# A two-layer encoder: the tail of each layer as one block per engine, norm root applied to the products, attention head by head

## The reference, cut to what matters

```python
def rms_norm(x, g):
    y = xf * lax.rsqrt(jnp.mean(jnp.square(xf), axis=-1, keepdims=True) + NORM_EPS)
    return y * g
def cross_attention(h, m, w_q, w_kv, w_o):
    q = (h @ w_q).reshape(B, T, XATTN_HEADS, XATTN_HEAD_DIM)
    ...
    p = jax.nn.softmax(einsum('bqhd,bkhd->bhqk', q, k) * (XATTN_HEAD_DIM ** -0.5))
    return einsum('bhqk,bkhd->bqhd', p, v).reshape(B, T, D) @ w_o
...
    h = h + mixed @ w_out                                   # output projection of the mixer
    h = h + cross_attention(rms_norm(h, norm_xattn[i]), rms_norm(mem, norm_mem[i]), ...)
    h = h + jnp.square(jax.nn.relu(rms_norm(h, norm_ffn[i]) @ w_up)) @ w_down
```

## Time and profile before

| | us |
|---|---|
| median of 3 runs | 2164.2 (2164.2 to 2166.83) |
| the profiled execution | 2160.84 |
| its span in the trace | 2158.6 |
| tail of layer 0, from the end of its projection's products (363.14) to the end of the last down product (864.21) | 501.07 |
| the same of layer 1 (1638.37 to 2138.06) | 499.69 |

### The profile page before, as it was taken

The page is one execution under the profiler, slowest core; times in us unless marked ns, Lnnn a source line. Parts: engine busy times, 40 slices in busy tenths (PEclk is TensorE's granted clock), DMA queues, the critical chain, the costliest instruction groups (busy, mean ns, idle before and its releaser), DMA issues. The chain is left out here.

```text
span 2158.6 us, 40341 instructions
## 1 busy us (share of the span) xinstructions
PE 1953.0 (90%) x17897; PEld 1563.9 (72%) x17897; DVE 1092.0 (51%) x1403; ACT 760.1 (35%) x1023; POOL 208.0 (10%) x153
## 2 busy tenths in 40 slices
PE   6899878998999999899968888888688899999998
PEld 4798547766888888667747877888457677888886
DVE  4792554334432432565368787786264425423432
ACT  4422563333321321145543333332253424312322
POOL 1000001000000001220022222222010010000000
PEclk9999989999999999999979999999899999999998
DMA  5224323302233232343211111110423113332320
GB/s 174 85 69 148 120 79 117 98 20 78 92 104 98 79 117 78 116 159 119 101 50 35 36 36 36 35 33 18 165 87 117 59 40 90 105 98 79 97 98 39
DMA packets 153015, 183.76 MB, mean 85 GB/s; under 512 B 9033, under 2 KB 141302, under 8 KB 151306
## 3 DMA queue, kind: packets, MB, share of 16 engines
q1 hardware_dynamic: 148576, 168.28, 23.9%
q0 software_dynamic: 3616, 12.71, 1.5%
q10 hardware_dynamic: 650, 0.19, 0.0%
HBM read 160.18 MB, written 20.99 MB: 84 GB/s over the span
## 5 line engine op out<-in xcount | busy, mean ns | idle before, releaser
L327 DVE TENSOR_TENSOR weights_lo<-w,weights_hi 128x2048 fp32r<-128x2048 f32 x106 | 242.9, 2292 | 299.2 <-ACT weights_hi L314 299.2
L314 ACT ACTIVATE weights_hi<-w 128x2048 fp32r<-128x2048 f32 x110 | 210.5, 1913 | 212.0 <-PE ps L342 202.5
L340 PE MATMUL ps<-f_hn_hi,weights_hi 128*128 128x512 f32 x512 | 204.5, 399 | 11.5 <-DVE f_hn_lo L389 11.5
L341 PE MATMUL ps<-f_hn_lo,weights_hi 128*128 128x512 f32 x512 | 201.3, 393 | 0.0
L342 PE MATMUL ps<-f_hn_hi,weights_lo 128*128 128x512 f32 x512 | 201.0, 393 | 0.0
L340 PE MATMUL ps<-f_hidden_hi,weights_hi 128*128 128x512 f32 x512 | 199.7, 390 | 0.0
L341 PE MATMUL ps<-f_hidden_lo,weights_hi 128*128 128x512 f32 x512 | 199.2, 389 | 0.0
L342 PE MATMUL ps<-f_hidden_hi,weights_lo 128*128 128x512 f32 x512 | 199.2, 389 | 0.0
L340 PEld LDWEIGHTS ps<-f_hn_hi,weights_hi 128*128 128x128 f32 x512 | 97.3, 190 | 41.1 <-issue 13.1
L1348 DVE TENSOR_TENSOR f_squared<-f_relu 128x512 f32<-128x512 f32 x64 | 44.3, 692 | 161.5 <-ACT f_relu L1325 161.5
L340 PE MATMUL ps<-x_hn_hi,weights_hi 128*128 128x512 f32 x256 | 102.3, 400 | 14.9 <-DVE x_hn_lo L389 11.5
(11 more groups left out here) (369 smaller groups left out, 3861.4 us busy)
## 6 DMA issues: line engine op xcount, KB each, us to landing
w<-in_ffn_w_up_dram SPq DMA_DIRECT2D x32, 1024.0 KB, 5.5
w<-in_ffn_w_down_dram SPq DMA_DIRECT2D x32, 1024.0 KB, 5.1
w<-in_xattn_w_kv_dram SPq DMA_DIRECT2D x16, 1024.0 KB, 5.5
w<-in_ab_w_in_dram SPq DMA_DIRECT2D x10, 1024.0 KB, 5.8
w<-in_xattn_w_q_dram SPq DMA_DIRECT2D x8, 1024.0 KB, 5.2
w<-in_xattn_w_o_dram SPq DMA_DIRECT2D x8, 1024.0 KB, 5.1
w<-in_ab_w_out_dram SPq DMA_DIRECT2D x4, 1024.0 KB, 5.1
w<-in_rwkv_w_r_dram SPq DMA_DIRECT2D x4, 1024.0 KB, 6.7
```

The lines of the kernel that those rows point to most:

```text
L314: act.activation(hi, raw, ACT.Copy).then_inc(k.w_hi_ready, 1)
L327: eng.tensor_tensor(lo, raw, hi.bitcast(F32), ALU.subtract).then_inc(k.w_lo_ready, 1)
L340: pe.matmul(out, lhs[0], rhs[0], start=start, stop=False)
L341: pe.matmul(out, lhs[0], rhs[1], start=False, stop=False)
```

## The change

- The three stages become one block, `stage_layer`; buffers are placed by hand so that all fit.
- The norm's input is `h * gain` without the root (`Stream`). ACT rounds it straight from `h` and squares the same chunk; DVE takes the rest. This is done for chunk c as soon as DVE has added it to `h`.
- The root is applied later. DVE multiplies it in when it empties a bank of queries (ACT did that before, without a root) and when it takes the ReLU of an up chunk (ACT's before). ACT now squares twice, once in full and once rounded.
- The attention goes head by head. PE's queue is written as the string `order` below: Q is a chunk of queries, S scores and T transposes of a unit (now two blocks of 128 tokens of one head), O an output chunk, and X01-23 the share of input chunks 2 and 3 in output chunks 0 and 1 of the projection. X0 to X2 gather in banks 4 to 6.
- Keys and values of the memory are fetched by POOL's queue during the output projection; they were fetched by SP's at the start of `stage_cross`.
- In the up phases the round and the rest of a slot are written one step apart as before, but ACT's round stands behind the odd chunk instead of the next even one.

The lines that go are the three functions printed above. Of the new ones the core is:

```diff
+
+    def chunk(self, act, c):
+
+        k = self.k
+        act.activation(self.pair.hi[:, c, :], k.h[:, c, :], ACT.Copy, scale=k.p(self.gain, self.g0 + c)) \
+           .then_inc(self.pair.s_hi, 1)
+        self.squares.square(act, c)
+
+    def rest(self, dve, c):
+
+        k, pair = self.k, self.pair
+        dve.wait_ge(pair.s_hi, self.base + c + 1)
+        dve.scalar_tensor_tensor(pair.lo[:, c, :], k.h[:, c, :], k.p(self.gain, self.g0 + c),
+                                 pair.hi[:, c, :].bitcast(F32), ALU.mult, ALU.subtract).then_inc(pair.s_lo, 1)
+
+    def wait(self, pe, c):
+
+        pe.wait_ge(self.pair.s_lo, self.base + c + 1)
+
+    def root(self, act, tmp):
+
+        warm_ln(self.k, act)
+        rstd_act(self.k, act, self.k.ps[:, 7, :], self.squares.stats(), tmp, self.rs, 1.0 / D, self.s_rs)
...
+    tmp, rs = sq[:, 2, :], sq[:, 3, :]
+    co = a_pair
+    s_rs, s_k, s_v, s_mx, s_pn, s_xf, s_xd, s_r2 = (
+        k.sem(f"x{l}_" + n) for n in ("rs_ready", "keys_in", "values_in", "max", "probs", "first_summed", "first_added",
+                                      "hidden_squared"))
+    squares = [Squares(k, sq, tmp) for _ in range(3)]
+    hx = Stream(k, b_pair, 0, "norm_xattn", 8 * l, squares[0], rs, s_rs)
+    hf = Stream(k, b_pair, C, "norm_ffn", 8 * l, squares[1], rs, s_rs)
+
+
+    order = """Q0 Q1 +0 Q2 Q3 S0 S1 Q4 T0 S2 Q5 T1 S3 O0 O1 Q6 T2 S4 Q7 T3 S5 O2 O3 X01-01 T4 S6 X01-23 T5 S7 O4 O5 T6
+               X2-0123 T7 X01-45 O6 O7 X2-45 X3-01 X01-67 X3-234567 X2-67""".split()
...
+    ends = [num["o%d" % n] for n in (1, 3, 5, 7)] + [num["Q%d" % n] for n in (1, 3, 5, 7)] \
+        + [(s_xf, 2), num["X3"], num["X5"], num["X7"]]
...
+    def attended(eng, c):
+
+        if c < 3:
+            eng.wait_ge(s_xd, c + 1)
+        else:
+            k.wait_freed(eng, num["X%d" % c])
+
+    def first_bank(c):
+        return k.ps[:, 4 + c, :]
...
+            mm3_first(pe, k, num["Q0"], ws, b_pair.both, lambda c: hx.wait(pe, c), WQ)
+            for kind, arg in order[2:]:
+                j = num.get(kind + arg)
+                if kind == "+":
+                    squares[0].sum(pe)
+                elif kind == "Q":
...
+                        m = pe.matmul(k.bank(j), vv[:, c, n * P:(n + 1) * P], pt[:, h % 2, c, :],
+                                      start=(c == 0), stop=(c == 1))
+                    m.then_inc(k.done(j), 1)
+                else:
+                    outs, chunks = arg.split("-")
+                    if arg == "01-01":
+                        ws.wait(pe, WX)
+                    elif arg == "2-0123":
+                        ws.wait(pe, WX + 1)
+                    elif arg == "3-01":
+                        k.take(pe, num["X3"])
+                    for c in (int(x) for x in chunks):
+                        k.wait_freed(pe, num["O%d" % c])
+                        for n in (int(x) for x in outs):
+                            bank = first_bank(n) if n < 3 else k.bank(num["X3"])
+                            m = mm3(pe, bank, ws.pair(WX + n // 2, c, slice(n % 2 * P, (n % 2 + 1) * P)),
+                                    [x[:, c, :] for x in co.both], c == 0, c == 7)
+                            if c == 7:
+                                m.then_inc(s_xf if n < 3 else k.done(num["X3"]), 1)
+            for n in range(4, C):
+                if n % 2 == 0:
+                    ws.wait(pe, WX + n // 2)
...
+                    mm3_first(pe, k, up[0], ws, b_pair.both, lambda c: hf.wait(pe, c), WF)
+                    squares[1].sum(pe)
...
+            for c in range(C):
+                k.wait_freed(act, num["o%d" % c])
+                hx.chunk(act, c)
+                if c % 2:
+                    ws.round(act, c // 2 + 2)
+            hx.root(act, tmp)
+
+            for kind, arg in order:
+                j = num.get(kind + arg)
+                if kind == "Q" and int(arg) % 2:
+                    ws.round(act, WQ + int(arg) // 2 + 2)
...
+                elif kind == "O":
+                    n = int(arg)
+                    k.wait_full(act, j)
+                    co.round(act, n, k.bank(j))
+                elif arg == "01-67":
+                    ws.round(act, WX + 2)
+            for c in range(C):
+                attended(act, c)
+                hf.chunk(act, c)
+                if c >= 3 and c % 2:
+                    ws.round(act, WX + c // 2 + 2)
+            hf.root(act, tmp)
...
+                for n in range(H):
+                    x = half * H + n
+                    k.wait_freed(act, up[half] + n)
+                    if x >= 2:
+                        act.wait_ge(hid.s_lo, x - 1)
+                    act.activation(r2[:, n % 2, :], rl[:, n % 2, :], ACT.Square).then_inc(s_r2, 1)
+                    act.activation(hid.hi[:, n, :], rl[:, n % 2, :], ACT.Square).then_inc(hid.s_hi, 1)
+                    if n % 2:
+                        ws.round(act, WF + half * NS + n // 2 + 2)
...
+            scored = None
+            for kind, arg in order:
+                j = num.get(kind + arg)
+                if kind in "QTX" and scored is not None:
+                    probs(scored)
+                    scored = None
+                if kind == "Q":
+                    n = int(arg)
+                    if n == 0:
+                        dve.wait_ge(s_rs, 1)
+                    k.wait_full(dve, j)
+                    if n >= 4:
+                        k.wait_full(dve, num["S%d" % (2 * (n // 2 - 2) + 1)])
+                    dve.scalar_tensor_tensor(qt[:, n // 2 % 2, n % 2, :], k.bank(j), 1.0 / 16, rs, ALU.mult, ALU.mult) \
+                       .then_inc(k.free(j), 1)
+                    if n % 2:
+                        ws.rest(dve, WQ + n // 2 + 2)
...
+                elif kind == "O":
+                    n = int(arg)
+                    dve.wait_ge(co.s_hi, C + n + 1)
+                    dve.tensor_tensor(co.lo[:, n, :], k.bank(j), co.hi[:, n, :].bitcast(F32), ALU.subtract) \
+                       .then_inc(k.free(j), 1)
+                elif arg == "01-67":
+                    ws.rest(dve, WX + 2)
...
+            dve.wait_ge(s_rs, 2)
+            for half in range(2):
+                for n in range(H + 1):
+                    if n < H:
+                        x = half * H + n
+                        k.wait_full(dve, up[half] + n)
+                        if x >= 2:
+                            dve.wait_ge(hid.s_hi, x - 1)
+                        dve.scalar_tensor_tensor(rl[:, n % 2, :], k.bank(up[half] + n), 0.0, rs, ALU.max, ALU.mult) \
+                           .then_inc(k.free(up[half] + n), 1)
+                    if n:
+                        dve.wait_ge(s_r2, half * H + n)
+                        hid.rest(dve, n - 1, r2[:, (n - 1) % 2, :], half * H + n)
                         if n % 2 == 0:
...
+                            ws.rest(dve, WF + half * NS + n // 2 + 1)
...
+        def _(pool):
+            pool.wait_ge(a_pair.s_lo, C)
+            pool.dma_start(kt[:, :, :], k.d_kt[l]).then_inc(s_k, 16)
+            pool.dma_start(vv[:, :, :], k.d_vv[l]).then_inc(s_v, 16)
+            for s in squares:
+                s.add(pool)
+    k.stats = squares[2].stats()
```

548 lines of the change are left out of this document (231 added, 317 removed).

## The result

| | before | after |
|---|---|---|
| median of four runs, us | 2164.2 (2163.7 to 2166.8) | 2103.0 (2101.2 to 2105.3) |
| the profiled execution, us | 2160.84 | 2102.36 |
| its span, us | 2158.6 | 2100.2 |

The ratio is 0.9715, with an interval of 0.9699 to 0.9732. The time is 61.2 us shorter.

A forecast was written before the change was run, and what follows sets the result against it. PE, busy 90% of the span, was taken as the bound, so gains lie where it idles or runs slowly. Layers of 472.6 us against 501.07 and 499.69 give 55.6 off 2164.2: 2108.6 us, range 2101 to 2124.

The forecast's parts named there:

- norm roots: Ahead of queries and up phase: 8.47 us gap and half clock go per norm, 1.7 us of sum comes.
- attention: Attention of each layer: 31.6 us of PE's bare work plus 1.5 of waits, where before took 40.71.
- slot change: Up phases: PE's wait for weights_lo at slot changes goes, 1.2 us for each of two halves, both layers.
- walk: Queues walked by durations; attention waits 1.5 us a layer, bounds 0 and 9.1; 2103 to 2115 us, chance 0.76.
- Rival 4: Roots stay on the path because first query and up banks need them: 23 us more, 2131; chance 0.04.
- Point (a): Behind query chunk 3: DVE's chain takes 7.6 us, PE reaches T0 after 8.9 and doesn't wait.
- Point (b): Behind query chunks 5 and 7: ACT rounds before copying transposes; PE waits 0.75 us twice, before O0 and O2.
- (c): At output chunk O7: round and rest need 1.7 us; X2-45 and X3-01 last 2.7.
- (d): In the projection: X4's slot is split in 4.6 us behind X01-67; 24 matmuls between take 5.45.
- Rival 1: Attention stays bound by hand-offs, earlier waits return spread over heads: 13.8 us more, 2122; chance 0.12.
- Rival 3: Up phases: DVE rests weights late, PE waits at slots from 1.5 us of delay; 126 us more, 2235; chance 0.03.
- Rival 2: Attention: clock falls at short waits, once a head; 16 us plus 7 of waits, 2132; chance 0.05.

The follow-up runs named there:

- uncovered order: Changed kernel with each head's scores, transposes and outputs written with no weight products between and the projection behind all heads: 2158.89 us, ratio 0.9969.
- uncovered orders: The uncovered order (2158.89 us), and the same with the attention's weight rounds and rests moved behind the output chunks: 2148.62 us, ratio 0.9929.

## Why the prediction was right, point by point

**Where the time went.** The tails took 57.7 us less, predicted 55.6. By parts, in us for both layers:

| part | predicted | measured | by |
|---|---|---|---|
| norm roots and half clock behind them, less the sums | 37.1 | 35.4 | root back on the path |
| attention | 13.8 | 14.3 | stretches: 40.71 and 39.33 before, 32.8 and 32.9 after |
| slot change | 4.8 | 5.3 | the edit alone in the kernel before |
| rest | 0 | 2.7 | difference to 57.7 |

The prediction's 37.1 is 2 x 8.47 + 2.3 + 2.7 - 2 x 1.7 for a layer, twice. After's 32.8 is the time from the first query to the end of the projection, 121.55, less 1.7 for the sum and less 2 x 43.52. The rest of 2.7 was not isolated by a run, but the stretches of before and after place nearly all of it. By them alone the norms come to 37.5 us: four gaps of 8.47, the half clock in the queries (2.4 and 2.8 over 43.52) and in the first up phases (2.7 and 2.5 over the second), less four sums of 1.7. The slot change comes to 5.8 and the projection to 0.2, which with the attention's 14.3 makes 57.8 of 57.7. The kernel with the root back falls short of 37.5 in part because its gaps are made differently (8.20 us). The one with the slot's change moved falls short of 5.8 because the first up phase of its layer 1 lost more to the half clock. Of the attention's 14.3 us 1.7 are the fall of the clock in layer 0, which is not there in every execution.

**The 5.6 us by which the forecast was high** are 2.1 from the tails, 0.7 from outside them, and 2.8 from the step from one execution to the median. The kernel before has its profiled execution 3.4 below its median; after's is 0.6 below. A single profiled execution stands that far from the median by chance, so the sum is no more exact than some 3 us. The walk's own lower bound, with the 1.5 us of waits at 0, would have been 2105.6; 2103.0 is under it, and inside the range only because the range was drawn down to 2101 without a term for it.

**Norm roots: right.** The input chunks were ready in time, and the root was hidden with 6.7 us to spare (predicted 6.5). The term for the sum, 1.7 us, was exact. Rival 4 fell with it.

**Attention: right, a little high.** Bare work 31.6 and waits 1.5 were predicted, 33.1; measured were 32.8, of which the waits cost 1.4 (listed as 0.94). Point (a) held: T0 came with no wait. Its chain of round, rest and probabilities took 7.3 us from the end of chunk 3 (386.7 to 394.05), predicted 7.6. Point (b) named both waits and the engine. The listed wait was lower: ACT's round and copy took 2.8 us from the chunk's end (403.26 to 406.06) instead of 2.95, and PE's work ahead of the wait 2.3 instead of 2.2. Points (c) and (d) held; no wait is seen there. Rival 1 did not come: the chains last as long as before, but products lie over them. With these taken away the heads cost 56 us more than after, while the old order, with its eight scores in a row, had cost only 14 more. The gain is the interleaving; head by head by itself would have been a loss.

**Up phases: right.** 87.04 was measured where 87.2 was taken. Rival 3's threshold was right as well: 1.4 us more per chunk cost nothing in the steady state, and 2.86 cost 1.34 at each slot change. The cover is only 1.5 us wide, and moving the round back (25 us) takes away two fifths of the gain. Rival 3's price of 126 us was far too high for that edit: with round and rest a chunk later, a change costs 1 us, not 3.95 at each of 32, since DVE's rest then starts as soon as the round is done and not a whole chunk later.

**Rival 2: the mechanism exists, the price was too low.** The changed kernel shows none of it, with PEclk 1.00 through both tails. In the uncovered order the clock falls in each head, by 3.1 us a fall where the prediction had 2. The Trainium skill, page "TensorE: Matmul & The Clock Gate", section "A second HAM failure mode: psum-queue depth-cycling", says of a kernel that cycles PSUM banks that small idles between groups of matmuls make the clock go back and forth. The uncovered orders agree (PEclk 0.75 to 0.87 with waits of 2.0 to 4.3 us). After, with some 20 switches and two listed waits of 0.47 us a layer, does not show it. The attention of the kernel before, with a wait of 2.84 us, kept the clock once in layer 1 and lost it there in the kernel with the slot change moved.

**Switches between split and plain products**, by which the sum could have failed, cost next to nothing. In layer 0 the queries, attention and projection together are within 0.25 us of their bare parts plus the two waits (1.7 + 87.04 + 31.6 + 0.94 = 121.3, or 121.7 with the waits at their cost of 1.4; measured 121.55) with some 20 switches.

## What to carry to other kernels

A factor that holds for a whole column of the output (here the root of a norm) can be put on when the products' banks are emptied; its chain then leaves the matmul path, provided that the first emptied bank is asked for later than the chain ends, which is the number to check. Short hand-off chains of an attention are hidden by products from neighbouring stages, and each such walk should list, per hand-off, what the product ahead covers and what queued work of ACT and DVE stands before the hand-off. Where the cover is thin, as with 1.5 us at a slot change here, the order in which two engines' housekeeping is written is worth more than the work in it.

## What the runs showed of the hardware

- The clock can fall at waits of 2.0 us (PEclk 0.76 and 0.87 in heads with one such wait and some of 0.5 to 0.8), and can stay at 1.00 through a wait of 2.84 us in another order. The same instructions with the same waits kept it in layer 1 of the kernel before (1.00) and lost it in layer 1 of the kernel with the slot change moved (0.96). So neither a wait's length nor the order decides alone.
- A fall cost about 3.1 us in the uncovered heads, 1.7 in the attention of layer 1 (41.02 against 39.33), and about 2.2 in front of the queries (24.03 against 21.8).
- A down phase of 384 products took 87.22 us before and 87.04 after, with no wait shown in either. With the slot's change of the up phase moved alone, it was 87.04 too, though no line of the down phase was edited.
